# Seven block products instead of eight for the first down projection of a two-layer decoder trunk

## The reference, cut to what matters

```python
def swiglu(x, w_gate, w_up, w_down):          # hidden width 2816 = 22 tiles of 128
    return (silu(x @ w_gate) * (x @ w_up)) @ w_down

for layer in range(2):
    h = conv_sgu_mixer(x, ...) if layer == 0 else dilated_attention_mixer(x, ...)
    x = layer_norm(ALPHA * x + h)
    x = layer_norm(ALPHA * x + swiglu(x, w_gate[layer], w_up[layer], w_down[layer]))
```

## Time and profile before

| | us |
|---|---|
| median of three runs | 1354.97 (1354.69 to 1356.37) |
| the profiled execution, own time | 1356.42 |
| its span, first to last instruction | 1354.6 |
| TensorE busy | 1341.0 (99%) |
| VectorE busy | 940.1 (69%) |
| ScalarE busy | 642.9 (47%) |
| GpSimd busy | 435.1 (32%) |

### The profile page before, as it was taken

The page is one execution under the profiler, slowest core; times in us unless marked ns, Lnnn a source line. Parts: engine busy times, 40 slices in busy tenths (PEclk is TensorE's granted clock), DMA queues, the critical chain, the costliest instruction groups (busy, mean ns, idle before and its releaser), DMA issues.

```text
span 1354.6 us, 20715 instructions
## 1 busy us (share of the span) xinstructions
PE 1341.0 (99%) x8055; PEld 1195.8 (88%) x8055; DVE 940.1 (69%) x1219; ACT 642.9 (47%) x997; POOL 435.1 (32%) x240
## 2 busy tenths in 40 slices
PE   8999999999999999999999999999999999999997
PEld 7887899999988889888888888888889999999885
DVE  3997598888866456777542767644238888889977
ACT  4465555554543343333422334333446455556566
POOL 4785600000054445555544535354242000000002
PEclk9999999999999999999999999999999999999999
DMA  9322224334353325777375776545222434335653
GB/s 272 93 95 85 71 68 120 93 102 115 95 176 105 94 62 162 193 189 187 95 218 147 178 191 164 130 142 148 55 62 76 112 93 113 103 93 202 202 181 123
DMA packets 197083, 176.23 MB, mean 130 GB/s; under 512 B 10293, under 2 KB 163657, under 8 KB 196840
## 3 DMA queue, kind: packets, MB, share of 16 engines
q1 hardware_dynamic: 182648, 156.59, 38.7%
q0 software_dynamic: 7744, 14.42, 6.1%
q10 hardware_dynamic: 6624, 4.29, 1.3%
HBM read 171.04 MB, written 33.08 MB: 151 GB/s over the span
## 4 chain that ended last, share of the span: by engine, by line
PE 97%; ACT 1%; DVE 1%; DMA 1%; issue 0%; SPq 0%; DVEq 0%; ACTq 0%
PE pq L1135 10%; PE pq L1134 10%; PE pq L1132 10%; PE pq L824 9%; PE pq L825 9%; PE pq L826 9%; PE pq L846 8%; PE pq L847 8%; PE pq L848 8%; PE pq L1330 3%; PE pq L1328 3%; PE pq L1329 3%; PE pq L1307 1%; PE pq L1266 1%; PE pq L1279 1%; PE pq L1300 1%
## 5 line engine op out<-in xcount | busy, mean ns | idle before, releaser
L707 POOL TENSOR_TENSOR w_lo<-stage,w_hi 128x1024 fp32r<-128x1024 f32 x132 | 327.0, 2482 | 573.5 <-ACT w_hi L1401 573.5
L1401 ACT ACTIVATE w_hi<-stage 128x1024 fp32r<-128x1024 f32 x173 | 179.1, 1053 | 199.4 <-PE pq L848 126.3
L824 PE MATMUL pq<-xt_hi,w_hi 128*128 128x512 f32 (+1 forms) x624 | 228.4, 366 | 0.5 <-DVE xt_lo L1930 0.4
L826 PE MATMUL pq<-xt_hi,w_lo 128*128 128x512 f32 (+1 forms) x624 | 225.2, 361 | 0.0
L825 PE MATMUL pq<-xt_lo,w_hi 128*128 128x512 f32 (+1 forms) x624 | 225.2, 361 | 0.0
L1134 PE MATMUL pq<-xt_lo,w_hi 128*128 128x256 f32 x632 | 178.9, 283 | 0.0
L1135 PE MATMUL pq<-xt_hi,w_lo 128*128 128x256 f32 x632 | 178.9, 283 | 0.0
L1132 PE MATMUL pq<-xt_hi,w_hi 128*128 128x256 f32 x632 | 178.8, 283 | 0.0
L715 POOL TENSOR_TENSOR x_res<-x_res,norm_b 128x512 f32<-128x512 f32 x24 | 30.4, 1292 | 338.7 <-ACT x_res L1435 337.2
L824 PEld LDWEIGHTS pq<-xt_hi,w_hi 128*128 128x128 f32 x624 | 117.9, 189 | 19.6 <-DVE xt_lo L1930 1.2
L826 PEld LDWEIGHTS pq<-xt_hi,w_lo 128*128 128x128 f32 x624 | 117.8, 189 | 18.0
(11 more groups left out here) (287 smaller groups left out, 2915.7 us busy)
## 6 DMA issues: line engine op xcount, KB each, us to landing
stage<-in_od_w_qkv_dram SPq DMA_DIRECT2D x72, 512.0 KB, 4.4
stage<-in_ffn_w_gate_dram SPq DMA_DIRECT2D x44, 512.0 KB, 4.9
stage<-in_ffn_w_up_dram SPq DMA_DIRECT2D x44, 512.0 KB, 4.0
stage<-in_ffn_w_down_dram SPq DMA_DIRECT2D x33, 512.0 KB, 3.5
stage<-t_rows SPq DMA_DIRECT2D x27, 512.0 KB, 3.3
t_rows<-in_ffn_w_down_dram SPq DMA_DIRECT2D x22, 512.0 KB, 7.4
stage<-in_ev_w_in_dram SPq DMA_DIRECT2D x16, 512.0 KB, 5.5
t_rows<-in_ffn_w_down_dram POOLq DMA_DIRECT2D x11, 512.0 KB, 7.9
```

The source lines that it names most:

```text
L707: pool.tensor_tensor(w_lo[slab % RING][:, :], w_stage[slab % RING][:, :], w_hi[slab % RING][:, :].bitcast(F32), ALU.subtract).then_inc(w_l ...
L824: pe.matmul(o, hi[:, k, :], x_hi, start=(k == 0), stop=False)
L826: last = pe.matmul(o, lo[:, k, :], x_hi, start=False, stop=(k == KD - 1))
L1401: act.activation(w_hi[slab % RING][:, 0:width], w_stage[slab % RING][:, 0:width], ACT.Copy).then_inc(w_hi_ready, 1)
```

## The change

The first down projection also goes by blocks: row tiles 0 to 15 in 8 pairs by seven products each (`PAIRS = (8, 11)`), tiles 16 to 21 as six whole rows behind them. `down_lay` gives the order: 16 slabs with two block sums each, 2 front rows, 4 slabs with `four` sums, 6 rows, 6 whole rows, 34 slabs in all. VectorE makes their low parts; GpSimd makes none in this stage.

The block sums: SP issues the copies of pairs 0 to 5 behind its loads of slabs 8, 10, 12, 15, 17 and 19, and those of pairs 6 and 7 between the last up tile and the positions. GpSimd issues two accumulating DMAs behind each of slabs 16 to 23 and 16 more once the last unit's sum is made, from the fourth on one for each high part of a slab of the projection. The `four` sums of layer 1 now lie in four whole and three half slabs, where they lay in five whole and one half, so there are 7 of these slabs and 29 in the projection instead of 28. `rot_tmp` gets memory of its own.

```diff
+PAIRS = (8, KF // 2)
+SUM4_WHOLE = 4
+COPY_BEHIND = (8, 10, 12, 15, 17, 19)
+SUMS_FROM = 16
+EARLY_SUMS = ((BOTH, 0), (OWN, 0), (BOTH, 1), (OWN, 1), (THREE, 0), (BOTH, 2), (OWN, 2), (THREE, 1),
+              (BOTH, 3), (OWN, 3), (THREE, 2), (BOTH, 4), (OWN, 4), (THREE, 3), (BOTH, 5), (OWN, 5))
+LATER_SUMS = ((THREE, 4), (THREE, 5), (BOTH, 6), (OWN, 6), (BOTH, 7), (OWN, 7), (THREE, 6), (THREE, 7),
+              *((FOUR, j) for j in range(PAIRS[0])))
...
             for slab in range(RING + 4, S_UP0):
                 load(slab)
+                if slab in COPY_BEHIND:
+                    copy_blocks(0, COPY_BEHIND.index(slab))
...
+                for n in range(end):
+                    if n == 2:
+                        load_ln(e, layer, 1)
+                    if n < rest and n % 2 == 0:
+                        sp.wait_ge(t_three[layer][n // 2 % 2], 16 * (n // 4 + 1))
+                    elif n == fours:
+                        sp.wait_ge(t_four, 16 * sum(PAIRS[:layer + 1]))
+                    load(first + n)
...
             load_up(S_UP0, 0)
+            for j in range(len(COPY_BEHIND), PAIRS[0]):
+                copy_blocks(0, j)
...
             for slab in range(S_UP0):
                 split_low(slab)
+                for step, j in EARLY_SUMS[2 * max(slab - SUMS_FROM, 0):2 * max(slab - SUMS_FROM + 1, 0)]:
+                    block_sum(0, step, j)
                 if slab == 17:
...
+            pool.wait_ge(s31_set, UNITS)
+            for n, (step, j) in enumerate(LATER_SUMS):
+                if n >= 3:
+                    pool.wait_ge(w_hi_ready, plain(S_DOWN0 + n - 3) + 1)
+                block_sum(0, step, j)
...
-                    blocks_next = layer and static == UNITS - 2
+                    blocks_next = static == UNITS - 2
                     if blocks_next:
                         split_high(down)
                     high_s3(u + 1)
```

## The result

The changed kernel takes 1361.86 us (median of 5 runs, 1360.65 to 1363.81) beside 1354.87 for the kernel before (5 runs, 1354.59 to 1356.37). The ratio is 1.0053, 95% interval [1.0042, 1.0064]: slower by 0.5%, 0.9 us outside the predicted range.

What follows compares the result with a forecast made beforehand. TensorE, busy nearly all the span, was taken as the bound. -10.9 + 0.65 + 4.3 + 6.4 + 1.0 + 0.8 = +2.25 us on the median 1354.97 gave 1357.2 us, with an 8-in-10 range of 1350.3 to 1361.

Steps and rivals of the forecast that it cites:

- The saving: First down projection: 480 matmuls instead of 528, 48 fewer at 0.227 us each, -10.9 us.
- the block form's: First down projection: handing over between pairs and combining corners, as layer 1 shows, costs TensorE +0.65 us.
- GpSimd beside slabs 16 and 17: Convolution: four DMA issues delay GpSimd's chain, for which TensorE already waits, +4.3 us.
- SP's queue: Before the first projection: six copies ahead of slab 0 make it land at 380.4, TensorE loses +6.4 us.
- L - 373.95: Last unit before the projection: TensorE's loss when slab 0 lands at time L; 6.4 us at 380.4.
- Can't pass: SP's queue: each queue is served in ring order, so a load can't pass copies of its own queue; no separate size.
- GpSimd's issues beside VectorE: Projection's pairs: two sums issued per pair slow VectorE, which has little free time, +1.0 us (0 to 3).
- The case of L2540: VectorE instruction beside GpSimd's work: its durations were read as an issue slowing VectorE by 1.5 to 2, some 0.4 us.
- The tail of layer 1: Second projection's end: three half slabs instead of one crowd ScalarE's splits and delay the first norm step, +0.8 us.
- slower, from the same queue: Before the projection: slab 0 lands at 383 or later, TensorE loses 9 plus 1.5 for clock; 1361; two slower rivals together 0.35.

Runs made afterwards that it cites:

- all_in_ffn: Changed kernel with no copies ahead of slab 0, early sums from slab 18, last sixteen sums issued during the feed-forward's up part: 1345.66 us, ratio 0.9931.
- sums_from_17: Changed kernel with GpSimd's block sums beginning behind slab 17 instead of 16, the displaced ones after the first norm: 1359.26 us, ratio 1.0029.
- sums_from_18: Changed kernel with GpSimd's block sums beginning behind slab 18 instead of 16, the four displaced ones after the first norm: 1356.87 us, ratio 1.0013.
- the last two kernels: all_in_ffn, 1345.66 us, and the same kernel with the second down projection's `four` slabs laid out as before, 1345.65 us, ratio 0.9925.
- slab0_ahead: Changed kernel with the load of slab 0 issued right behind the last up load, ahead of the copies of pairs 6 and 7: 1357.68 us, ratio 1.0013.
- both_early: Changed kernel with the edits of copies_early and sums_from_18 together: 1347.99 us, ratio 0.9944.
- copies_early: Changed kernel with the copies of pairs 6 and 7 issued behind slabs 14 and 21, none ahead of slab 0: 1353.63 us, ratio 0.9989.
- one_set_early: Changed kernel with only one of the two copy sets moved from ahead of slab 0, to behind slab 14: 1353.59 us, ratio 0.9987.
- slab0_last: Changed kernel with layer 0's split of slab 0 moved behind the last unit's `d` (low part behind the corner), copies staying: 1356.87 us, ratio 1.0013.

## Why the prediction was wrong, step by step

The number was 1357 and the time is 1361.86. Of the costs in its sum all were there but one (VectorE slowed by issues), both large ones were sized too small, and the fall of TensorE's clock, which both have behind them, wasn't in the sum.

- **The saving**, -10.9, with **the block form's** +0.65: -10.25 was forecast and the projection is 10.13 shorter, in all_in_ffn 10.14. Right.
- **GpSimd beside slabs 16 and 17**, +4.3: the delay is 3.90, the loss 5.10. That TensorE had no slack there, so that the delay comes through one for one, was right and is what sums_from_17 shows. Two things were off. The printed durations of the issues overstate them (two take 1.28 us from start to start, 98.06 to 99.34, not 2.14), while the next instruction behind them is longer: L829 takes 3.52 us, against 2.71 where nothing is issued ahead of it (sums_from_18). And the clock's fall, 1.20, which the prediction had only in its slower rival and for the other place, isn't in the term.
- **SP's queue**, +6.4: 10.59. This is the step that failed. Slab 0 was put at 380.4 on the clock of before; it lands at 387.1, which less the 4.8 us of the first loss is 382.3. The formula "L - 373.95" then gives 8.4, and TensorE's wait is 8.5. The low part of `s3` comes at L + 2.4, as forecast, but the path is another: TensorE stops two products earlier, at `difference`, for `u_kept`, which the prediction doesn't have and which lets it go on at L + 4.9. `d`, which was to be the last to come, at L + 7.5 with the corner, has its low part at L + 7.2 (L2318, 393.06 + 1.22) and TensorE doesn't wait for it. `difference` and `remainder_21` in between take 2.88 us at the full clock, so both paths let `remainder_12` begin at nearly the same time; that the formula holds is luck in this. The landing was built from 12 us for the first set and 5.3 for the second. With one set slab 0 lands 10.0 us after the first copy and with two 19.0 (18.8 to 19.8 in the three other kernels with this order): the first set was put 2.0 too high, and the second, taken at the rate of the copies that ran alone, 5.3, cost 9.0, 3.7 more. What of that is due to the positions and GpSimd's sums beside it, no run separates. So TensorE's wait was 2.1 us longer than the 6.4, and the other half of the miss is the clock, 10.59 - 8.5 = 2.1 us, which this term put at nothing; the prediction had it only in its slower rival.
- The sentence on the Trainium skill (DMA: Bandwidth & Descriptors, Queues, rings and completion order), that each ring of a queue is served in order, fits the traces: ahead of the copies slab 0 lands after 4.8 us, behind them after 11.9, and in the change it lands 3.7 us behind the last copy of its own queue. "Can't pass" is more than the section says: it has the descriptors taken in ring order, but a later one may finish its write first. No run here shows that.
- **GpSimd's issues beside VectorE**, +1.0: 0.1 (111.22 - 121.35 = -10.13, against -10.25). The mechanism isn't there; VectorE's instructions are as long with issues beside them as without. The case of L2540 from which the factor was taken was misread, and the trace of the kernel before could have shown it. VectorE's and GpSimd's timelines:

```profile
527.78 4.77 POOL L707 TENSOR_TENSOR w_lo<-stage,w_hi 128x1024 fp32r<-128x1024 f32 x2 [11.61 <-ACT w_hi L1401]
530.85 2.78 DVE L2540 TENSOR_TENSOR qk<-qk,norm_g 32x1024 f32<-32x1024 f32 x1
532.47 1.16 POOL L785 DMA_DIRECT2D t_rows<-in_ffn_w_down_dram  x1
...
643.28 4.75 POOL L707 TENSOR_TENSOR w_lo<-stage,w_hi 128x1024 fp32r<-128x1024 f32 x2 [7.08 <-ACT w_hi L1401]
646.13 2.99 DVE L2540 TENSOR_TENSOR qk<-qk,norm_g 32x1024 f32<-32x1024 f32 x1
```

The low parts end at 532.55 and 648.03. The first L2540 has a low part beside it for 1.70 us and the issue for the remaining 1.08; the second has one for 1.90 and nothing for the remaining 1.09. What is left of the instruction behind the low part is as long beside the issue as beside nothing. The Trainium skill (GPSIMD Engine Reference, Specifications) speaks of contention in SBUF's interfaces; taken for issues, it would have given the term's upper end, and the trace is against that use of it. What there is in its place, 1.3 us once ahead of the third pair, when the projection's start isn't delayed anyway, comes from late slabs.
- **The tail of layer 1**, +0.8: +0.68 in the change, 0.70 between the last two kernels. Right.
- The sum of what was measured: -0.27 + 5.10 + 10.59 - 10.13 + 0.16 + 0.68 = +6.13. The rival "slower, from the same queue" had +6.3 and 1361, with a landing from 383 on and the clock's fall in it; it decided at a landing of 381, and the landing was 382.3. It was the right story, at too low a chance, and the range that ended at its own value left no room for a clock that falls twice. That its total nearly fits is in part luck: it has 9 + 1.5 for the queue, where 8.5 + 2.1 were measured, and the +1.0 for VectorE, which isn't there, stands in for the clock at the convolution.

## What to carry to other kernels

A new wait of TensorE can cost more than its length: here single waits of 4.0 to 9.2 us cost 1.6 to 2.8 us on top, to be seen in the granted clock of the windows behind them, and shorter ones cost it in some places and not in others. The instruction that the waits' view names is only the last link: in the change it was `u_kept`, in slab0_ahead the hidden block, and what was late was a slab whose split stood on ScalarE ahead of them. A DMA has to be costed by what is ahead of it in its own queue at that moment, with the traffic that is there, and not by the rate of the same DMA alone; moving work to a stretch where the engine or queue is idle anyway (here GpSimd's 198 us between the first norm and the projection) won 5.0 us with the four sums that stood in front of the convolution's last sum (sums_from_18) and 2.3 with the last (all_in_ffn beside both_early). When the first, large wait is mended, the next in the same place appears: read the projection again after each step.

## What the runs showed that was not expected

- The clock. After waits of 1.7 and 2.0 us with two us of work between them it fell to 0.50 in the change, in copies_early, one_set_early and slab0_last, and didn't in slab0_ahead; one wait of 1.9 us (sums_from_17) left it at 1.00, and so did waits of 1.7, 2.3 and 1.3 us within 17 us at the start of slab0_last's projection; single waits of 4.0 (slab0_ahead), 8.2 (sums_from_18), 8.5 (the change) and 9.2 us (sums_from_17) brought it down each time. The Trainium skill (TensorE: Matmul & The Clock Gate, Part 1) has the two levels and a gate that closes after idleness, and these traces have both; which of the waits of about 2 us bring the clock down, they don't settle.
- GpSimd's arithmetic right behind its own DMA issues takes 0.7 to 0.8 us longer: L829 3.52 us against 2.71, L821 2.04 against 1.30.
- GpSimd's issues leave VectorE's two-input instructions at 1220 and 951 ns.
- Two sets of copies (2.5 MB) ahead of a load make it land 19.0 us after the first was issued, one set 10.0, none 3.2 us after the load's own issue. A load can be as late without copies: slab 2 of copies_early takes 10.1 us from issue to landing, with GpSimd's sums going on, while in all_in_ffn, without them, the median of the slabs there is 3.3.
